# GpSimd's scale and shift of x waits for both token tiles of the next input to be split

## The chip, the cores and the metric

One core of one Trainium2 chip. The metric is the device time of the whole kernel in microseconds (us), one launch, inputs and result in HBM.

## The reference

Two layers, each of three sublayers, over x of 256 tokens by 1024 features, fp32. The six sublayers s = 0 to 5 are a gated feed-forward ("ffn"), a hybrid of window attention and a gated linear scan ("hyb"), ffn, ffn, a latent attention ("mla"), ffn. Each is wrapped like this, with shift, scale and gate out of a matrix product of a condition vector with `ada_w`:

```python
def modulated_sublayer(x, mod, g, b, fn, res_w):
    shift, scale, gate = mod[:, 0, None, :], mod[:, 1, None, :], mod[:, 2, None, :]
    y = fn(x * (1.0 + scale) + shift)
    return layer_norm(DEEPNORM_ALPHA * x + res_w * (1.0 + gate) * y, g, b)
```

The kernel makes each fp32 product out of three: each operand is split into a high part (rounded) and a low part (the rest), and high*high, low*high and high*low are summed.

## The kernel before

**Tiling.** The 256 tokens are two tiles of 128 (t = 0, 1). The weights come in slots of 128 x 2048 numbers: SyncE issues the loads into a ring of three raw buffers, ScalarE writes the high part (L771), VectorE the low part (L1042), TensorE uses both, over a ring of six. An ffn walks 11 column blocks of the hidden layer (c0 = 0 to 10), three slots each: `up` makes gate and up, VectorE multiplies (L1384, `hidden`), TensorE turns the product (`turn`, L1808), ScalarE and VectorE split it (L827 and L1389, `take_lo`), `down` adds to the result in PSUM.

**The order of the work is written out by hand, per engine.** Every engine has its own program, in one fixed order, and semaphores join them. An instruction that waits holds back all that stands behind it on its engine.

**Between two sublayers.** For each token tile, VectorE does `residual` (L1109, L1113) and `norm` (L1122 to L1128); within it GpSimd takes the power for the standard deviation (L591). L1128 leaves the normalised x in place, without the layer norm's g and b. TensorE transposes this (L1471), and VectorE (L1067) and ScalarE (L785) apply g, b, scale and shift in one step, folded into mod_G and mod_B. ScalarE rounds to hT_hi (L790, two halves), VectorE subtracts to hT_lo (L1075, two halves of 128x512), and each half raises `h_ready` by 1. The next sublayer's products wait for h_ready. VectorE's order is: residual and norm of tile 0, `enter` of tile 0 (L1067, L1075), residual and norm of tile 1, `enter` of tile 1.

**GpSimd's scale and shift.** x itself is needed with g and b as well, for the residual one sublayer later. GpSimd does that in `ln_tail`: x times ln_g (L599), plus ln_b (L601), 128x1024 each and in place, per tile; L601 raises `x_ready`. It must not start before TensorE has transposed the tile (`n_tr`).

**What stands behind ln_tail on GpSimd's queue.** Behind s = 0: masks for hyb (L628 to L649), then the distances (L655) as soon as SyncE's `mixer_inputs` have landed. Those loads (L512 to L519) wait for `x_ready` on SyncE's queue, and further weight loads stand behind them. ScalarE's L939 takes the absolute value of the distances; on ScalarE it stands ahead of the copy of the second projection's last piece (L953), and TensorE's next transposes (L1640) wait for that copy. Behind s = 1 and s = 2: `acc_start` (memset L556, bias load L559), then the loads of `ada_w` pieces (L545) into a ring of four. VectorE adds them up (L1054) from c0 = 1 on, two pieces ahead of a `split_lo` and a `take_lo`. Behind s = 3: 16 memsets for the frequencies of the rotation (L720); VectorE computes angles from them (L1263 to L1285), ScalarE the sines (L867), and behind that on ScalarE stand the squares (L871), for VectorE's and GpSimd's norms. Behind s = 4: the loads of ln_g and ln_b of the last sublayer.

Of the kernel before, what the change touches and what calls it, by code (L numbers as in the profile page):

```python
# [25 lines left out]
NT = SEQ // P  # L26
# [17 lines left out]
def build(nc, A, out):  # L44
# [11 lines left out]
    with ExitStack() as ctx:  # L56
# [3 lines left out]
        def sem(name):  # L60
            return ctx.enter_context(nc.semaphore(name))
# [129 lines left out]
        n_ready = sem("n_ready")  # L191
        n_tr = sem("n_tr")
# [3 lines left out]
        h_ready = sem("h_ready")  # L196
        pool_step = sem("pool_step")
        ln_rows_in = sem("ln_rows_in")
# [337 lines left out]
        def _(pool):  # L536
# [39 lines left out]
            def ln_tail(s):  # L576

                l, sub = divmod(s, N_SUB)
                if subs[s][0] == "hyb":

                    pool.wait_ge(ho_done, 8)
                elif subs[s][0] == "mla":

                    pool.wait_ge(o_ready, O0 + 4)
                for v, w in enumerate((A["ln_g"], A["ln_b"])):
                    pool.dma_start(ln_rows[:, v, :], w[l, sub:sub + 1, :].broadcast_to([P, D]))\
                        .then_inc(ln_rows_in, 16)
                for t in range(NT):
                    u = 2 * s + t
                    pool.wait_ge(var_ready, u + 1)  # L590
                    nc.gpsimd.tensor_tensor(rstd[:, :], var_eps[:, :], neg_half[:, :], ALU.pow).then_inc(rstd_ready, 1)  # L591
                    pool.wait_ge(n_ready, u + 1)
                    if s < last_sub:
                        pool.wait_ge(n_tr, 2 * (u + 3))
                    elif t == NT - 1:

                        break
                    pool.wait_ge(ln_rows_in, 32 * (s + 1))
                    step(nc.gpsimd.tensor_tensor(x[:, t, :], x[:, t, :], ln_rows[:, 0, :], ALU.mult))  # L599
                    step.wait()  # L600
                    nc.gpsimd.tensor_tensor(x[:, t, :], x[:, t, :], ln_rows[:, 1, :], ALU.add).then_inc(x_ready, 1)  # L601
                if s < last_sub:
                    pool.wait_ge(x_ready, 2 * (s + 1))

            for s, (kind, _, _) in enumerate(subs):
# [16 lines left out]
                if kind == "hyb":  # L622
# [57 lines left out]
                    for stage, m in hybrid_plan():  # L680
# [11 lines left out]
                        elif stage == "cum":  # L692
                            d, t = HSTEP[m]
# [3 lines left out]
                        elif stage in ("prod", "turn"):  # L697
                            d, t = HSTEP[m]
# [17 lines left out]
                if kind == "mla":  # L716
# [19 lines left out]
                    for stage, m in mla_plan():  # L736
                        if stage == "cn":
                            t = m
# [3 lines left out]
                        elif stage == "kr":  # L742
                            t = m[1]
# [6 lines left out]
                        elif stage == "uq":  # L750
                            g, t = m
# [5 lines left out]
                            x_rope = q_nat[:, t, :, 64:96]  # L757
                            rotate(x_rope, t, q_rot, [x_rope])
                ln_tail(s)


# [1149 lines left out]
```

## Time and profile before

| | |
|---|---|
| time, median of 3 runs (lowest, highest) | 1282.5 us (1280.75, 1288.55) |
| profiled execution: span from first to last instruction | 1283.1 us |
| TensorE matmul busy | 1144.7 us (89%) |
| VectorE busy | 823.9 us (64%) |
| ScalarE busy | 485.9 us (38%) |
| GpSimd busy | 234.8 us (18%) |
| TensorE's mean granted clock | 0.929 |

The profiled execution has no time of its own beside the span, so the span stands for it. Busy is the time in which an engine's instructions ran. The granted clock is a share of full speed. L12 is line 12 of the kernel; PE is TensorE, DVE is VectorE, ACT is ScalarE, POOL is GpSimd, SP is SyncE.

### The profile page before, as it was taken

To read this page: it belongs to the slowest core of one execution; us is meant where nothing else is said; L and a number is where in the kernel's file an instruction comes from. 1 tells how busy PE (TensorE), PEld (TensorE's weight loads), DVE (VectorE), ACT (ScalarE), POOL (GpSimd) and SP (SyncE) were. 2 spreads that over 40 slices of the span, in tenths; PEclk is the share of its full clock that TensorE was granted. 3 is DMA by queue.
4 is the path that set the end of the run, shared out by engine and by line. 5 is a ranking of instruction groups with operands and counts; after the bars stand their busy time and mean duration, and the time that the engine had idled before them with its cause. 6 is when DMAs were issued, how large, how long until landed. Compare 5 with 4: busy or idle time off the path is not lost. (4 is left out here: it accounts for less than half of the span.)

```text
span 1283.1 us, 14861 instructions
## 1 busy us (share of the span) xinstructions
PE 1144.7 (89%) x5205; PEld 916.4 (71%) x5205; DVE 823.9 (64%) x930; ACT 485.9 (38%) x666; POOL 234.8 (18%) x341
## 2 busy tenths in 40 slices
PE   1799999969988788999998899999889887999995
PEld 1688778747765456788787688888667676788883
DVE  6588688755565316796446799489565738444554
ACT  0543334325672103343443334343235533443440
POOL 0111221044232113210000411111143103000001
PEclk9999899879987768999999899999779998999997
DMA  8799889715451110897555399599114331665630
GB/s 317 263 318 375 299 315 357 247 31 170 132 164 52 47 33 33 312 369 275 164 191 196 125 370 356 206 364 353 41 58 148 99 99 59 204 197 197 197 98 33
DMA packets 145098, 252.28 MB, mean 197 GB/s; under 512 B 10386, under 2 KB 102802, under 8 KB 145043
## 3 DMA queue, kind: packets, MB, share of 16 engines
q1 hardware_dynamic: 124336, 176.98, 41.1%
q0 software_dynamic: 20560, 74.05, 15.4%
q8 instruction: 32, 0.52, 0.2%
q10 hardware_dynamic: 146, 0.53, 0.1%
q14 instruction: 24, 0.19, 0.0%
HBM read 250.48 MB, written 1.05 MB: 196 GB/s over the span
## 5 line engine op out<-in xcount | busy, mean ns | idle before, releaser
L1042 DVE TENSOR_TENSOR w_lo<-w_raw,w_hi 128x2048 fp32r<-128x2048 f32 (+2 forms) x164 | 364.5, 2226 | 150.8 <-ACT w_hi L771 150.6
L1476 PE MATMUL bank<-w_hi,hT_hi 128*128 128x512 f32 (+3 forms) x944 | 391.4, 415 | 32.6 <-DVE hT_lo L1075 25.0
L1479 PE MATMUL bank<-w_hi,hT_lo 128*128 128x512 f32 (+3 forms) x944 | 375.8, 398 | 0.0
L1480 PE MATMUL bank<-w_lo,hT_hi 128*128 128x512 f32 (+3 forms) x944 | 375.6, 398 | 0.0
L771 ACT ACTIVATE w_hi<-w_raw 128x2048 fp32r<-128x2048 f32 (+2 forms) x164 | 303.1, 1854 | 41.0 <-DMA w_raw<-in_ffn_w_up_dram 31.3
L1476 PEld LDWEIGHTS bank<-w_hi,hT_hi 128*128 128x128 f32 x944 | 187.2, 198 | 75.2 <-DVE hT_lo L1075 27.4
L1480 PEld LDWEIGHTS bank<-w_lo,hT_hi 128*128 128x128 f32 x944 | 185.9, 197 | 38.4
L1479 PEld LDWEIGHTS bank<-w_hi,hT_lo 128*128 128x128 f32 x944 | 187.2, 198 | 36.3 <-issue 2.3
L823 ACT ACTIVATE arena<-bank 128x256 f32<-128x256 f32 x88 | 33.8, 384 | 385.6 <-PE bank L1480 385.6
L1054 DVE SCALAR_TENSOR_TENSOR arena<-arena,cond 128x1024 f32<-128x1024 f32 x120 | 149.5, 1279 | 17.0 <-DMA arena<-in_ada_w_dram 16.9
L1476 PE MATMUL bank<-w_hi,fT_hi 128*128 128x512 f32 x352 | 143.1, 406 | 11.8 <-DVE fT_lo L1389 11.6
L1480 PE MATMUL bank<-w_lo,fT_hi 128*128 128x512 f32 x352 | 142.3, 404 | 0.0
L1479 PE MATMUL bank<-w_hi,fT_lo 128*128 128x512 f32 x352 | 141.9, 403 | 0.0
L545 POOL DMA_DIRECT2D arena<-in_ada_w_dram x120 | 63.5, 529 | 280.0 <-DVE arena L1054 254.1
L1384 DVE TENSOR_TENSOR arena<-arena,bank 128x256 f32<-128x256 f32 x88 | 36.9, 419 | 117.5 <-ACT arena L823 117.3
L1476 PEld LDWEIGHTS bank<-w_hi,fT_hi 128*128 128x128 f32 x352 | 69.0, 196 | 29.7 <-DVE fT_lo L1389 13.7
L591 POOL TENSOR_TENSOR rstd<-var_eps,neg_half 128x1 f32<-128x1 f32 x12 | 6.7, 559 | 417.4 <-DVE var_eps L1126 417.4
L1480 PEld LDWEIGHTS bank<-w_lo,fT_hi 128*128 128x128 f32 x352 | 68.9, 196 | 14.9
L1479 PEld LDWEIGHTS bank<-w_hi,fT_lo 128*128 128x128 f32 x352 | 68.9, 196 | 14.4
L827 ACT ACTIVATE fT_hi<-bank 128x256 fp32r<-128x256 f32 x88 | 33.7, 383 | 80.0 <-PE bank L1808 80.0
L1389 DVE TENSOR_TENSOR fT_lo<-bank,fT_hi 128x256 fp32r<-128x256 f32 x88 | 36.8, 418 | 21.3 <-ACT fT_hi L827 21.3
L1075 DVE TENSOR_TENSOR hT_lo<-arena,hT_hi 128x512 fp32r<-128x512 f32 x24 | 43.5, 1835 | 2.3 <-ACT hT_hi L790 1.0
(204 smaller groups left out, 958.3 us busy)
## 6 DMA issues: line engine op xcount, KB each, us to landing
arena<-in_ada_w_dram POOLq DMA_DIRECT2D x128, 512.0 KB, 6.1
w_raw<-in_ffn_w_gate_dram SPq DMA_DIRECT2D x88, 512.0 KB, 4.8
w_raw<-in_ffn_w_up_dram SPq DMA_DIRECT2D x88, 512.0 KB, 5.8
w_raw<-in_ffn_w_down_dram SPq DMA_DIRECT2D x88, 512.0 KB, 4.8
w_raw<-in_hyb_w_in_dram SPq DMA_DIRECT2D x26, 512.0 KB, 4.8
arena<-in_ada_w_dram SPq DMA_DIRECT2D x16, 512.0 KB, 5.3
w_raw<-in_hyb_w_out_dram SPq DMA_DIRECT2D x8, 512.0 KB, 4.0
w_raw<-in_mla_w_out_dram SPq DMA_DIRECT2D x8, 512.0 KB, 4.0
```

The lines of the kernel that those rows point to most:

```text
L545: pool.dma_start(ada_raw[:, a % ADA_RING, :], ada[l, :, k + 4 * i, sub * 3 * D + v * D:sub * 3 * D + (v + 1) * D])\
L771: nc.scalar.activation(w_hi[:, j0 % RING, 0:n], w_raw[:, j0 % RAW, 0:n], ACT.Copy).then_inc(hi_ready, 1)
L823: nc.scalar.activation(sg[:, t, :], G[t][:, 0:CW], ACT.Silu).then_inc(silu_done, 1)
L827: nc.scalar.activation(fT_hi[:, t, :], T[t][:, 0:CW], ACT.Copy).then_inc(fT_hi_ready, 1)
L1042: nc.vector.tensor_tensor(w_lo[:, j0 % RING, 0:n], w_raw[:, j0 % RAW, 0:n], w_hi[:, j0 % RING, 0:n].bitcast(F32), ALU.subtract)\
L1054: nc.vector.scalar_tensor_tensor(out=acc[:, v * D:(v + 1) * D], in0=ada_raw[:, a % ADA_RING, :], scalar=cond[:, 1, bass.ds(k + 4 * i, 1)], ...
L1075: nc.vector.tensor_tensor(hT_lo[:, ks, t * P:(t + 1) * P], scratch[:, half * 512:half * 512 + 512].rearrange("p (k n) -> p k n", k=4), hT_ ...
L1384: nc.vector.tensor_tensor(hid[:, t, :], sg[:, t, :], G[t][:, CW:2 * CW], ALU.mult)\
L1389: nc.vector.tensor_tensor(fT_lo[:, t, :], T[t][:, 0:CW], fT_hi[:, t, :].bitcast(F32), ALU.subtract).then_inc(fT_ready, 1)
L1476: mm = nc.tensor.matmul(dst, a_hi, b_hi, start=start, stop=False)
L1479: nc.tensor.matmul(dst, a_lo, b_hi, start=False, stop=False)
L1480: return nc.tensor.matmul(dst, a_hi, b_lo, start=False, stop=stop)
```

## The change

In `ln_tail` both powers (L591) now come first, for both tiles; then come the wait for ln_g and ln_b, and the two scale-and-shift pairs. Ahead of each pair GpSimd waits for h_ready >= 2 * (2s + 4), which is the second half of tile 1's hT_lo of the next sublayer. The last sublayer keeps its old wait.

```diff
@@ -589,13 +589,16 @@
                     u = 2 * s + t
                     pool.wait_ge(var_ready, u + 1)
                     nc.gpsimd.tensor_tensor(rstd[:, :], var_eps[:, :], neg_half[:, :], ALU.pow).then_inc(rstd_ready, 1)
-                    pool.wait_ge(n_ready, u + 1)
+                pool.wait_ge(ln_rows_in, 32 * (s + 1))
+                for t in range(NT):
+                    u = 2 * s + t
                     if s < last_sub:
-                        pool.wait_ge(n_tr, 2 * (u + 3))
+                        pool.wait_ge(h_ready, 2 * (2 * s + 4))
                     elif t == NT - 1:
 
                         break
-                    pool.wait_ge(ln_rows_in, 32 * (s + 1))
+                    else:
+                        pool.wait_ge(n_ready, u + 1)
                     step(nc.gpsimd.tensor_tensor(x[:, t, :], x[:, t, :], ln_rows[:, 0, :], ALU.mult))
                     step.wait()
                     nc.gpsimd.tensor_tensor(x[:, t, :], x[:, t, :], ln_rows[:, 1, :], ALU.add).then_inc(x_ready, 1)
```

## Rows read from the trace of the kernel before

**Rows 1.** All instructions of L1075: duration ns min/median/max, first and last start:

```profile
L1075 DVE TENSOR_TENSOR hT_lo<-arena,hT_hi x24: 681/1510/2862, 40.4 to 1084.1; 128x512 fp32r<-128x512 f32 x24
```

**Rows 2.** Timeline, entry of tile 0 into sublayer 1: start us, us, engine, line:

```profile
265.37 1.51 DVE L1075 TENSOR_TENSOR hT_lo<-arena,hT_hi 128x512 fp32r<-128x512 f32 x1
...
265.37 4.30 DVE L1075 TENSOR_TENSOR hT_lo<-arena,hT_hi 128x512 fp32r<-128x512 f32 x2
...
266.06 0.63 ACT L790 ACTIVATE hT_hi<-arena 128x512 fp32r<-128x512 f32 x1
...
263.99 2.34 POOL L599 TENSOR_TENSOR x<-x,arena 128x1024 f32<-128x1024 f32 x1 [3.91 <-issue]
266.41 2.71 POOL L601 TENSOR_TENSOR x<-x,arena 128x1024 f32<-128x1024 f32 x1
```

**Rows 3.** Timeline, sublayer 1's start, engine by engine (brackets: idle before, releaser):

```profile
280.48 0.58 PE L1476 MATMUL bank<-w_hi,hT_hi 128*128 128x256 f32 x1 [3.09 <-DVE hT_lo L1075]
...
279.61 0.63 ACT L790 ACTIVATE hT_hi<-arena 128x512 fp32r<-128x512 f32 x1
...
282.67 0.34 SPq L512 DMA_DIRECT2D arena<-in_hgrn_lb_logits_dram  x1
...
290.40 1.42 POOL L655 TENSOR_TENSOR arena<-arena,pos_col 128x256 int32<-128x256 int32 x2 [2.81 <-DMA arena<-in_hgrn_norm_w_dram]
...
294.35 0.62 ACT L939 ACTIVATE arena<-arena 128x512 f32<-128x512 int32 x1
297.49 0.60 ACT L953 ACTIVATE arena<-bank 128x512 f32<-128x512 f32 x1 [2.52 <-PE bank L1480]
...
298.14 1.10 PE L1640 MATMUL bank<-ident,arena 128*128 128x128 f32 x8 [0.69 <-ACT arena L953]
```

**Rows 4.** Timeline, GpSimd and VectorE at one time in sublayer 1:

```profile
299.92 3.23 DVE L1042 TENSOR_TENSOR w_lo<-w_raw,w_hi 128x2048 fp32r<-128x2048 f32 x1 [1.54 <-ACT w_hi L771]
...
298.47 5.84 POOL L668 TENSOR_TENSOR arena<-arena 128x512 f32<-128x512 f32 x3 [0.63 <-DVE arena L1140]
```

**Rows 5.** Timeline, sublayer 2's start, and L545's DMA issues between 510 and 540 us:

```profile
507.32 1.09 PE L1471 MATMUL bank<-ident,x 128*128 128x128 f32 x8 [0.32 <-DVE x L1128]
...
514.17 4.48 DVE L1042 TENSOR_TENSOR w_lo<-w_raw,w_hi 128x2048 fp32r<-128x2048 f32 x2
...
510.97 2.73 POOL L601 TENSOR_TENSOR x<-x,arena 128x1024 f32<-128x1024 f32 x1
...
517.53 0.55 POOL L545 DMA_DIRECT2D arena<-in_ada_w_dram  x1 [0.21 <-issue]
...
528.48 2.48 DVE L1054 SCALAR_TENSOR_TENSOR arena<-arena,cond 128x1024 f32<-128x1024 f32 x2
...
533.08 0.42 DVE L1389 TENSOR_TENSOR fT_lo<-bank,fT_hi 128x256 fp32r<-128x256 f32 x1
...
535.89 0.39 PE L1476 MATMUL bank<-w_hi,fT_hi 128*128 128x512 f32 x1
...
DMA to landing us min/median/max: 4.8/5.6/9.0
```

**Rows 6.** Timeline, sublayer 3's start (TensorE, VectorE):

```profile
716.24 1.09 PE L1471 MATMUL bank<-ident,x 128*128 128x128 f32 x8 [1.17 <-DVE x L1128]
...
737.12 2.48 DVE L1054 SCALAR_TENSOR_TENSOR arena<-arena,cond 128x1024 f32<-128x1024 f32 x2
```

**Rows 7.** Timeline, sublayer 4's (mla) start, engine by engine:

```profile
940.38 0.59 POOL L720 MEMSET freq<- 128x1 f32 x16
...
943.76 0.26 ACT L867 ACTIVATE rot<-angle 128x64 f32<-128x64 f32 x1 [5.84 <-DVE angle L1285]
...
950.40 1.22 DVE L1042 TENSOR_TENSOR w_lo<-w_raw,w_hi 128x1024 fp32r<-128x1024 f32 x1
...
953.78 1.97 PE L1541 MATMUL bank<-ident,arena 128*128 128x128 f32 x8 [0.28 <-DVE kr_nat L1305]
```

**Rows 8.** Windows of TensorE: stretch, its length, busy, granted clock (0.50 means 1.2 GHz):

```profile
498.80:504.10 5.30, 5.29 (x13) 0.50 0.00 0
```

## The prediction

> **What bounds the kernel now.** I read the busy shares first: TensorE's matmuls fill 89% of the span, so the time is TensorE's work plus the stretches in which it waits. The lines of the page name one wait above the others: L1476's first product of a sublayer waits for hT_lo (L1075). I then took L1075 by itself [rows 1]: 24 instructions of one shape take from 0.68 to 2.86 us, median 1.51. Equal work of such unequal length is waiting inside the instruction. The timeline of one entry shows on what [rows 2]: L1075's first half starts at 265.37 while L599 runs on GpSimd (to 266.33), and ends 0.55 us after that; then L601, which had started at 266.41, takes 2.71 instead of L599's 2.34, and the pair of L1075 ends at 269.67, 0.55 us after L601. The two engines take turns, each holding the other off for a whole instruction. The last view was the timeline of each of the five entries, for what stands behind `ln_tail` on GpSimd and when somebody waits for it [rows 3, 5, 7]. It decides this case.
>
> **Part one: hT_lo is freed.** With GpSimd idle L1075 costs its minimum, 0.68. The first half is ready 1.51 - 0.68 = 0.83 us earlier. The second half needs L790's second output (266.69), so it ends at 267.4 instead of 269.67: 2.27 us earlier, and VectorE goes on with tile 1's residual and norm that much sooner. What reaches TensorE differs by place:
> - Sublayer 1: TensorE waits for tile 1 anyway, so 2.27 arrive at tile 1's transposes and 0.83 more at its first product [rows 3]: 3.1 us.
> - Sublayer 2: TensorE is busy with `up` of tile 0 until 0.32 us before tile 1's transposes [rows 5]: 0.83 + 0.32 = 1.15. Tile 1's hT_lo is not waited for, since `down` comes between. Sublayer 4 repeats this pattern; there tile 1's first half (0.83) counts too.
> - Sublayer 3: idle 1.17 [rows 6]: 0.83 + 1.17 = 2.0.
> - Sublayer 5: about 0.8, only the first half.
> - The powers (L591) of both tiles ahead of the pairs cost nothing: they wait for VectorE in both orders.
>
> **Part two: GpSimd's four instructions move behind the second half of tile 1.** They are 4 x 2.34 us plus gaps, 9.8 us, where before only the second pair was left at that time. And they now meet VectorE's split of the next weight slots (L1042, 2.2 us each, two SBUF operands, 4.48 for two undisturbed [rows 5]). No row of before has this pair of shapes together; the nearest has L668, three instructions in 5.84 us, against one L1042 of 3.23 instead of 2.24 [rows 4]. So they take turns there as well: each w_lo that falls in lengthens GpSimd's series by up to 2.2. Bounds are 0 and 2.2 per w_lo; I take 2.2 where VectorE is ready.
>
> The Trainium skill (SBUF — State Buffer, Who interferes with whom) says that a VectorE instruction with two SBUF inputs and a GpSimd instruction that reads SBUF exclude each other for the whole instruction; a mere sharing of bandwidth would give the lower bound of each place below. The turns in the trace speak for the rule.
>
> Who waits behind these four:
>
> *Sublayer 1.* The last half of hT_lo ends at 280.24 - 2.27 + 0.7 = 278.7 (280.24 is L790's end [rows 3]). Four instructions and one w_lo bring x_ready to 290.5; before it was 282.64, just ahead of SyncE's L512 at 282.67 [rows 3]. So mixer_inputs start 7.8 us later; L655, which waited 2.81 us for them, comes at 298.2 and ends at 299.6. ScalarE's L939 had no wait (it ran at 294.35); now it stands at its place in ScalarE's order until 299.6. Behind it is L953, 0.5 us later, and TensorE's L1640 0.65 after L953's start: about 300.85 instead of 298.14. The gain of 3.1 is eaten, and 2.7 us are lost: **+2.7**. With no turns taken, x_ready is 2.2 earlier: +0.5.
>
> *Sublayer 2.* hT_lo's end: L1042 follows it at 514.17 now [rows 5]; less 1.15 and some 2.0 of lock wait, 511.1. Four instructions and three w_lo: 16 us, 527.1. From L601's end (513.70) to the first L545 (517.53) are 3.8 us of memset and bias load [rows 5], so the first piece is issued at 530.9 and lands 5.6 us later, at 536.5. VectorE wants it in L1054 at 528.48 now: 8.1 us late. L1389 stands behind, ends at 533.50, and TensorE takes its result at 535.89 [rows 5]: 2.4 us of cover. **+5.7** there, the entry's gain already counted. Bounds: landing 4.8 to 9.0 us gives +4.9 to +9.1; with no turns GpSimd is 6.2 earlier and little is left, about 0 to +1.
>
> *Sublayer 3* repeats it with a head start larger by 0.85 and L1054 at 737.12 [rows 6], 14.5 instead of 14.8 us after L601's end: 7.5 - 2.4 = **+5.1**. The second loop of pieces there, and the loads after the first four, are gated by VectorE's own progress and shift with it.
>
> *Sublayer 4.* The frequencies (L720) start as soon as ln_tail ends, 940.38 [rows 7]. VectorE's angles wait for them, ScalarE waited 5.84 us in front of L867 [rows 7], and squares, norms and the copies of kr stand behind that. No w_lo falls in. Against sublayer 1's 7.8, that is 2.2 less, and 1.2 more for the smaller head start (1.1 for 2.3): 6.8 us later. L1042 now ends at 951.62 [rows 7], then 958.4; with two short copies behind it, L1541 starts at 958.8 instead of 953.78: **+5.0**. VectorE is idle there, so this is the surest term.
>
> *Sublayer 5.* Nothing on GpSimd is wanted before 1268 us; the w_lo that are delayed have some 3 us in hand. **-0.8**.
>
> **The clock.** After an idle stretch TensorE ran 5.3 us at a granted clock of 0.50, 1.2 GHz [rows 8], which costs a stage bound by TensorE up to 2.5 us. Three of the new waits (sublayers 1 to 3) stand where it now runs at full clock; each costs between 0 and 2.5. I take half, **+3.6** in all, since VectorE is itself late behind two of them.
>
> **The sum.** 2.7 + 5.7 + 5.1 + 5.0 - 0.8 + 3.6 = 21.3 us, on the span of 1283.1, which is 0.6 above the median of the runs: 1282.5 + 21.3, so 1304.
>
> **Rivals.**
> - *The freed hT_lo is all that counts.* If nothing behind ln_tail is on a path, the entries give -3.1 - 1.15 - 2.0 - 1.9 - 0.8 = -9 us: 1273.5. For it: GpSimd is busy only 18%, and the waits removed are real. Against it: each of the rows L939, L867 and L1054 shows its engine with under 8 us in hand. The Trainium skill (same page, Summary: rules for kernel authors) advises to schedule whichever of the two is off the critical path; read for this change it would give this case. Chance 0.12.
> - *The second queue is covered, the others not.* GpSimd's series is not lengthened by w_lo, or pieces land early, so that sublayers 2 and 3 lose nothing: 0.5 + 0.5 + 0 + 5.0 - 0.8 = +5, 1288. For it: landing as short as 4.8 us, a cover of 2.4. Chance 0.13.
> - *It is worse.* Pieces land in 9 us (+3.4 twice) and each wait brings its full slow stretch (+3.9 more): 1315. Decides if the loads of weights fall together with the late pieces. Chance 0.10.
> - *The wait does nothing*, if GpSimd came late to it anyway: it starts L599 at 263.99 now, before the first half of tile 0 is even written [rows 2]. Chance 0.01.
>
> **How the numbers follow.** The forecast has 0.64, its own range 1297 to 1312. The range 1288 to 1316 takes in the covered and the worse case and leaves out the first rival. Of single runs (1280.75 to 1288.55) I hold that under 1% can't be told from no change. 1% slower is 1295.3: forecast and worse case, with a little of the edge taken off, 0.73. Within 1% are both milder cases, 0.25. Faster by 1% needs more than the first rival's 9 us: 0.02.
>
> **What the changed profile would show.** L1075's instructions near 0.7 us, save none. L599 and L601 in four, about 16 us, between 511 and 527 in sublayer 2, with L1042 stretched beside them. TensorE waiting some 6 us for ScalarE's L953 ahead of L1640, some 7 for L1389 at c0 = 1 in sublayers 2 and 3, and 5 to 7 ahead of L1541. VectorE's L1054 waiting for the piece's DMA near 8 to 9 us, twice. The prediction is wrong if L1054's wait is under 3 us, if L939 finds its input ready, or if GpSimd's four take 10 us in sublayer 2.

## The result and the profile after

The changed kernel takes 1307.9 us (median of 4 runs, 1301.0 to 1314.1), beside 1285.3 us for the kernel before in the same rounds (4 runs, 1280.75 to 1288.55). The ratio is 1.0171, with a 95% interval of 1.0132 to 1.021. The profiled execution has a span of 1307.8 us, 24.7 more than before; this section accounts for these 24.7. From L599 on the line numbers are 3 higher than before (L1075 is L1078 now).

First the wait that the change was to remove. This is the line of hT_lo, with what waited for it:

```profile
L1078 DVE TENSOR_TENSOR hT_lo<-arena,hT_hi x24: 680/692/693, 39.5 to 1108.2; 128x512 fp32r<-128x512 f32 x24
...
  POOL x L602: 32.9, 5
```

All 24 instructions take 0.68 to 0.69 us, none is held up any more (1.51 in the median before, [rows 1]). The second row is the price: GpSimd now stands idle 32.9 us in five waits in front of L602. The timeline of sublayer 1's start shows both:

```profile
264.04 0.58 PE L1479 MATMUL bank<-w_hi,hT_hi 128*128 128x256 f32 x1 [2.27 <-DVE hT_lo L1078]
...
276.79 2.37 POOL L602 TENSOR_TENSOR x<-x,arena 128x1024 f32<-128x1024 f32 x1 [6.59 <-DVE hT_lo L1078]
...
284.04 4.33 POOL L604 TENSOR_TENSOR x<-x,arena 128x1024 f32<-128x1024 f32 x1
...
283.32 2.79 DVE L1045 TENSOR_TENSOR w_lo<-w_raw,w_hi 128x2048 fp32r<-128x2048 f32 x1 [6.68 <-ACT w_hi L774]
...
288.40 0.34 SPq L512 DMA_DIRECT2D arena<-in_hgrn_lb_logits_dram  x1
...
296.07 2.13 POOL L658 TENSOR_TENSOR arena<-arena,pos_col 128x256 int32<-128x256 int32 x2 [1.42 <-DMA arena<-in_hgrn_norm_w_dram]
...
298.23 0.63 ACT L942 ACTIVATE arena<-arena 128x512 f32<-128x512 int32 x1 [8.93 <-POOL arena L658]
...
298.76 0.58 ACT L956 ACTIVATE arena<-bank 128x512 f32<-128x512 f32 x1
...
299.40 1.97 PE L1643 MATMUL bank<-ident,arena 128*128 128x128 f32 x8 [7.10 <-ACT arena L956]
```

TensorE's first product waits 2.27 instead of 3.09 [rows 3]. Then read the chain downward by its brackets. The last of the four instructions takes 4.33, because L1045 holds it off. SyncE's L512 follows at 288.40 (282.67 before), then GpSimd's distances, then ScalarE's L942, which waits 8.93 where it had not waited. L956 stands behind it, and TensorE waits 7.10 where it had waited 0.69 [rows 3].

Sublayer 2, the other queue:

```profile
513.57 2.38 POOL L602 TENSOR_TENSOR x<-x,arena 128x1024 f32<-128x1024 f32 x1 [7.26 <-DVE hT_lo L1078]
516.03 4.32 POOL L604 TENSOR_TENSOR x<-x,arena 128x1024 f32<-128x1024 f32 x1
520.32 4.44 POOL L602 TENSOR_TENSOR x<-x,arena 128x1024 f32<-128x1024 f32 x1
524.84 4.32 POOL L604 TENSOR_TENSOR x<-x,arena 128x1024 f32<-128x1024 f32 x1
529.22 2.68 POOL L556 MEMSET arena<- 128x3072 f32 x1
...
533.01 1.88 POOL L545 DMA_DIRECT2D arena<-in_ada_w_dram  x3 [0.22 <-issue]
...
514.53 7.97 DVE L1045 TENSOR_TENSOR w_lo<-w_raw,w_hi 128x2048 fp32r<-128x2048 f32 x2 [1.11 <-ACT w_hi L774]
...
537.28 2.48 DVE L1057 SCALAR_TENSOR_TENSOR arena<-arena,cond 128x1024 f32<-128x1024 f32 x2 [7.59 <-DMA arena<-in_ada_w_dram]
...
542.43 0.79 PE L1479 MATMUL bank<-w_hi,fT_hi 128*128 128x512 f32 x1 [5.18 <-DVE fT_lo L1392]
```

The four take 15.6 us (513.57 to 529.16) and the two w_lo 7.97 instead of 4.48 [rows 5]: the turns that L1075 was freed from are taken here. The pieces of ada_w are issued after that, VectorE waits 7.59 for the first, and TensorE 5.18 for the L1392 behind it. In sublayer 3 the same wait of L1057 is 6.58, and TensorE's behind it 3.78. Sublayer 4:

```profile
957.08 2.37 POOL L602 TENSOR_TENSOR x<-x,arena 128x1024 f32<-128x1024 f32 x1 [7.01 <-DVE hT_lo L1078]
...
966.72 0.59 POOL L723 MEMSET freq<- 128x1 f32 x16
...
970.10 0.26 ACT L870 ACTIVATE rot<-angle 128x64 f32<-128x64 f32 x1 [13.89 <-DVE angle L1288]
...
978.20 1.12 PE L1544 MATMUL bank<-ident,arena 128*128 128x128 f32 x4 [8.22 <-DVE kr_nat L1308]
```

No w_lo falls in, so these four take 9.6 us, but ScalarE waits 13.89 instead of 5.84 for the angles and TensorE 8.22 instead of 0.28 [rows 7].

**Where the 24.7 us lie.** I cut TensorE's time at the start of tile 0's transposes into each sublayer. The windows of after (stretch, its length, matmuls busy, granted clock):

```profile
260.70:496.74 236.04, 200.22 (x932) 0.81 0.27 90
496.74:715.79 219.05, 205.89 (x889) 0.94 0.64 221
715.79:940.55 224.76, 210.87 (x925) 0.95 0.73 259
940.55:1093.44 152.89, 123.00 (x648) 0.87 0.28 92
1093.44:1307.80 214.36, 190.15 (x852) 0.96 0.43 142
```

Before, the cuts lie at 262.78, 494.62, 703.57, 921.33 and 1067.13, with 196.70, 199.66, 207.75, 122.13 and 194.67 us busy. Length less busy is idle. The matmuls are the same in number (one record more or less), so a difference in busy time is a difference in clock:

| us against before | start | sub 1 | sub 2 | sub 3 | sub 4 | sub 5 | sum |
|---|---|---|---|---|---|---|---|
| TensorE idle | +0.1 | +0.7 | +3.9 | +3.9 | +6.2 | +2.9 | +17.7 |
| TensorE busy (clock) | -2.2 | +3.5 | +6.2 | +3.1 | +0.9 | -4.5 | +7.0 |
| both | -2.1 | +4.2 | +10.1 | +7.0 | +7.1 | -1.6 | +24.7 |

The stretch before the first cut runs the same code in every kernel of this study. Over the twelve other profiles it came out between 5.4 us shorter and 0.7 longer than before, most of it in the busy row (-5.9 to +0.2), and its idle row scatters by 2.7. The later stretches scatter too. Each of these ranges is over kernels that have the same code in that stretch: sublayer 1 with the old order came out at -2.6 to +0.6 against before, with the new order at +4.2 to +6.9; sublayer 3 with the new order at +7.0 to +11.5; sublayer 4 with the new order at +5.1 to +7.1. So a difference of under some 3 to 4 us between single profiles of one stretch shows nothing by itself.

### The profile page after: what moved, and what is told of

It reads as the page before. It is cut to its first block, busy times and chain, and to the rows that moved or that the text cites. A ratio compares the mean times of both kernels' runs of the same rounds, so it can differ in the third digit from the quotient of the medians.

```text
span 1307.8 us, 14855 instructions
## 1 busy us (share of the span) xinstructions
PE 1151.8 (88%) x5205; PEld 921.3 (70%) x5205; DVE 814.5 (62%) x930; ACT 486.4 (37%) x666; POOL 250.9 (19%) x341
## 4 chain that ended last, share of the span: by engine, by line
PE 62%; DVE 13%; issue 7%; ACT 7%; DMA 5%; POOL 5%; SPq 0%; DVEq 0%; POOLq 0%; ACTq 0%
PE bank L1479 17%; PE bank L1482 17%; PE bank L1483 17%; DMA arena<-in_ada_w_dram 4%; DVE w_lo L1045 3%; ACT w_hi L774 2%; POOL x L604 2%; POOL x L602 2%; PE bank L1456 2%; PE bank L1811 1%; PE bank L1750 1%; PE bank L1464 1%; DVE arena L1365 1%; PE bank L1753 1%; PE bank L1474 1%
## 5 line engine op out<-in xcount | busy, mean ns | idle before, releaser
L1045 DVE TENSOR_TENSOR w_lo<-w_raw,w_hi 128x2048 fp32r<-128x2048 f32 (+2 forms) x164 | 380.0, 2321 | 158.5 <-ACT w_hi L774 158.3
L1057 DVE SCALAR_TENSOR_TENSOR arena<-arena,cond 128x1024 f32<-128x1024 f32 x120 | 149.7, 1280 | 30.6 <-DMA arena<-in_ada_w_dram 30.6
L545 POOL DMA_DIRECT2D arena<-in_ada_w_dram x120 | 63.5, 529 | 268.1 <-DVE arena L1057 242.6
L591 POOL TENSOR_TENSOR rstd<-var_eps,neg_half 128x1 f32<-128x1 f32 x12 | 6.7, 557 | 435.8 <-DVE var_eps L1129 435.8
L1392 DVE TENSOR_TENSOR fT_lo<-bank,fT_hi 128x256 fp32r<-128x256 f32 x88 | 36.9, 419 | 23.4 <-ACT fT_hi L830 23.4
L1811 PE MATMUL bank<-ident,arena 128*128 128x128 f32 x176 | 35.8, 286 | 12.7 <-DVE arena L1387 12.6
```

Source lines behind the costliest of these rows:

```text
L545: pool.dma_start(ada_raw[:, a % ADA_RING, :], ada[l, :, k + 4 * i, sub * 3 * D + v * D:sub * 3 * D + (v + 1) * D])\
L1045: nc.vector.tensor_tensor(w_lo[:, j0 % RING, 0:n], w_raw[:, j0 % RAW, 0:n], w_hi[:, j0 % RING, 0:n].bitcast(F32), ALU.subtract)\
L1057: nc.vector.scalar_tensor_tensor(out=acc[:, v * D:(v + 1) * D], in0=ada_raw[:, a % ADA_RING, :], scalar=cond[:, 1, bass.ds(k + 4 * i, 1)], ...
L1392: nc.vector.tensor_tensor(fT_lo[:, t, :], T[t][:, 0:CW], fT_hi[:, t, :].bitcast(F32), ALU.subtract).then_inc(fT_ready, 1)
L1811: mm = nc.tensor.transpose(T[t][:, q * P:(q + 1) * P], hid[:, t, q * P:(q + 1) * P], ident[:, :])
```

## The experiments

All cuts of time below are made in this way, in one profile of each kernel; lines may be numbered a few higher. Whole times are given with the ratio and its interval where the kernel was run in rounds. Diffs are against the changed kernel, unless they say otherwise.

**No pairs.** The scale and shift of x are left out in sublayers 0 to 4; `x_ready` is raised after the wait.

```diff
                         pool.wait_ge(h_ready, 2 * (2 * s + 4))
+                    if s < last_sub:
+                        pool.sem_inc(x_ready, 1)
+                        continue
```

> Left out: GpSimd's scale and shift of x by ln_g and ln_b in sublayers 0 to 4 (x stays without them for the residual); x_ready is raised when the new wait is over. Theory Q (the loss is what is queued behind the four instructions on GpSimd): no time is spent in front of the queue, so only the freed hT_lo is left; against before -3.1 in sublayer 1, -1.2, -2.0, -1.9, -0.8 in 2 to 5, together -9 us, 1276. Theory W (the late wait itself, or the powers put first, costs something whatever GpSimd does after it): it stays slower than before, over 1290. Theory C (mostly TensorE's clock, which falls at other places from run to run): a total anywhere between 1276 and 1290, and the same stretches at half clock in sublayers 1 to 3 as in the changed kernel.

Measured: 1276.1 us, ratio 0.9932 (0.991 to 0.9954), so 8.7 us faster than before by the ratio. The new wait itself therefore costs nothing, and all the loss comes from the four instructions at their new place. The 8.7 us are near the 9 that the first rival had put on the freed hT_lo, but they don't show its worth alone: without the pairs nothing else on VectorE is held up by them either, and the queues behind them run earlier. By sublayers 1 to 5 the one profile gives -2.4, -1.0, +1.1, -1.7 and -1.0, which is not the forecast's pattern (-2.0 was expected in sublayer 3).

**Loads first.** In sublayers 2 and 3 the memset, the bias load and the first four ada_w loads are issued ahead of the pairs.

```diff
+                if s in (1, 2):
+                    nxt = ada_plan[s + 1][0]
+                    acc_start(nxt)
+                    pool.wait_ge(h_ready, 4 * s + 8)
+                    for n in range(ADA_RING):
+                        ada_piece(nxt, n, 0)
                 pool.wait_ge(ln_rows_in, 32 * (s + 1))
...
+                        if s in (2, 3) and loop == 0:
+                            for n in range(ADA_RING, 24):
+                                ada_piece(nxt, n % 12, n // 12)
+                            continue
```

> The changed kernel, with the memset, the bias load and the first four loads of ada_w pieces of sublayers 2 and 3 ahead of the four instructions instead of behind them. Theory Q: L1057's waits for the piece (7.6 and 6.6 us) go to under 1 us; sublayer 2 falls from +10.1 (against before, entry to entry) to between -1.2 and +1, sublayer 3 from +7.0 to between -2 and +1; sublayers 1 and 4 stay at +4.2 and +7.1; in all 1308 - 17, about 1291. Theory L (what hurts is that the split of the weights takes 8.0 instead of 4.5 us beside the four instructions): sublayers 2 and 3 stay above +4 each, total over 1300.

Measured: 1303.3 us, one run; about 1291 was expected. Sublayer 2 fell from +10.1 to 0.0, and VectorE's waits for pieces there from 7.6 to 1.1 us in all. That settles sublayer 2: the pieces, issued late, are its cost; w_lo is still stretched (6.69 us for two) and delays nobody that TensorE waits for. Sublayer 3 stayed at +7.2 (idle +2.8, clock +4.4). Part of this the experiment made itself, in its timeline:

```profile
720.12 2.65 POOL L556 MEMSET arena<- 128x3072 f32 x1
720.20 3.12 DVE L1141 TENSOR_SCALAR x<-x,mean_var,rstd 128x1024 f32<-128x1024 f32 x1 [0.67 <-POOL rstd L591]
...
723.38 1.97 PE L1484 MATMUL bank<-ident,x 128*128 128x128 f32 x8 [3.64 <-DVE x L1141]
```

The memset now starts right behind the second power and holds VectorE's normalisation off: 3.12 instead of 0.81 us, in front of the transposes. In sublayer 2 the same happens (3.13 us at 511.27), but TensorE is busy there and waits only 0.84.

**Frequencies first.** The 16 memsets of L723 go ahead of the pairs of s = 3.

```diff
+                if s == 3:
+                    for n in range(16):
+                        op = nc.gpsimd.memset(freq[:, n:n + 1], float(np.float32(10000.0) ** np.float32(-n / 16)))
+                    op.then_inc(freq_ready, 1)
                 pool.wait_ge(ln_rows_in, 32 * (s + 1))
```

> The changed kernel, with the 16 memsets of freq in sublayer 4 ahead of the four instructions. Theory Q: VectorE's angles and ScalarE's sines are on time, but the power for the norms (L743) still stands behind the four; it comes at the end of the series instead of 5.1 us after it. TensorE's wait ahead of its transposes of c falls from 8.2 to about 3 us, sublayer 4 from +7.1 to about +2; total about 1303. If the frequencies were not what held sublayer 4: no change there, the wait stays at 8.

Measured: 1311.0 us, one run; about 1303 was expected. TensorE's wait for kr_nat fell from 8.22 to 5.49 us, where about 3 was expected. Its timeline shows why it fell no further:

```profile
961.99 7.20 DVE L1270 TENSOR_SCALAR angle<-freq,arena 128x16 f32<-128x16 f32 x4
...
981.32 1.97 PE L1544 MATMUL bank<-ident,arena 128*128 128x128 f32 x8 [5.49 <-DVE kr_nat L1308]
```

The frequencies are now there in time and VectorE starts on the angles at once. But it now does so beside GpSimd's four instructions (961.98 to 971.6), and they hold it off: four small products of 128x16 take 7.20 us, where the kernel before needs 0.65, and the two of L1274 behind them 2.42 instead of 0.27. ScalarE still waits 12.02 us in front of L870 (13.89 in after). So the late frequencies can't be the larger part of the term: taking them away won 2.7 us of a wait that had grown by 7.9, and the pairs themselves, on VectorE's angles, keep most of the rest. By the table sublayer 4 gave +2.7 (idle +4.9, clock -2.2) instead of +7.1; with the code of after it gave +5.2 in "loads first" and +5.1 in "absolute value late" (waits for kr_nat 7.20 and 7.26), so 2.4 us or more are gained.

The total doesn't show it, since sublayer 1, whose code is that of after, came out at +6.8 instead of +4.2. Sublayer 2, also unchanged, repeated its +10.1 (idle +3.9, clock +6.2).

**Absolute value late.** ScalarE's L942 goes behind ScalarE's copies of q, and so no longer stands ahead of the copy L956.

```diff
-                        elif stage == "dist":
-                            act.wait_ge(diff_ready, 2)
-                            nc.scalar.activation(dist[:, :, :], dist[:, :, :].bitcast(I32), ACT.Abs).then_inc(dist_abs, 1)
...
+                            act.wait_ge(diff_ready, 2)
+                            nc.scalar.activation(dist[:, :, :], dist[:, :, :].bitcast(I32), ACT.Abs).then_inc(dist_abs, 1)
```

> The changed kernel, with ScalarE's absolute value of the distances moved behind its copies of q (stage qk), so that it no longer stands ahead of the copy of the second projection. Theory Q: TensorE's 7.1 us ahead of its transposes of q fall to under 1.5 us, and the stretch at half clock after them goes; sublayer 1 from +4.2 to about -2; total about 1302. If GpSimd's masks or SyncE's late weight load (slot 5) hold sublayer 1 by themselves, TensorE waits 4 us or more at its next use, and sublayer 1 stays above +2.

Measured: 1309.6 us, one run; about 1302 was expected. TensorE's timeline in sublayer 1:

```profile
293.94 1.09 PE L1642 MATMUL bank<-ident,arena 128*128 128x128 f32 x8 [0.69 <-ACT arena L953]
...
304.75 0.70 PE L1659 MATMUL bank<-arena 64*128 64x256 f32 x4 [3.80 <-DVE arena L1151]
```

The wait of 7.10 is gone, back at 0.69, so ScalarE's order was its cause. Half of it comes back 11 us later, at L1659, which needs VectorE's work on what this chain delivers. Sublayer 1 went to +0.6, where three profiles with the code of after gave +4.2, +6.8 and +6.9; -2 was expected. Sublayer 3 came out at +11.5, of which +6.3 is clock, with the code of after: again the scatter.

**Write only.** The pairs are replaced by four pairs of memsets of about their length, into ln_rows: same queue time, no reads. x keeps no scale and shift.

```diff
+                    if s < last_sub:
+                        for m in range(2):
+                            step(nc.gpsimd.memset(ln_rows[:, :, :], 0.0))
+                            step.wait()
+                            step(nc.gpsimd.memset(ln_rows[:, 0, 0:660], 0.0))
+                            step.wait()
+                        pool.sem_inc(x_ready, 1)
+                        continue
```

> The changed kernel, with GpSimd's four instructions of sublayers 0 to 4 replaced by memsets of about the same length into the space of ln_g and ln_b (x's scale and shift are left out). They read nothing from SBUF. Theory Q with turns: without reads VectorE's w_lo and these memsets run beside each other, so the series is 9.8 us and the two w_lo after the entry take 4.5 us. x_ready comes 2 us earlier (sublayer 1 about +2 against before instead of +4.2), the pieces of ada_w 6 us earlier in sublayer 2 and 4 to 5 in sublayer 3 (L1057's wait 7.6 falls to 1 to 3, so sublayer 2 is near -1 and sublayer 3 near 0 apart from the clock), and sublayer 4, where no w_lo falls in, keeps its +7. Theory S (the two engines share bandwidth, or the order on GpSimd alone counts): lengths as in the changed kernel, all four sublayers unchanged.

Measured: 1295.0 us, one run. The timeline of sublayer 2:

```profile
511.78 1.81 POOL L604 MEMSET arena<- 128x2048 f32 x1 [5.96 <-DVE hT_lo L1086]
512.77 4.50 DVE L1053 TENSOR_TENSOR w_lo<-w_raw,w_hi 128x2048 fp32r<-128x2048 f32 x2 [1.11 <-ACT w_hi L782]
...
521.46 0.65 POOL L606 MEMSET arena<- 128x660 f32 x1
...
532.01 1.29 DVE L1065 SCALAR_TENSOR_TENSOR arena<-arena,cond 128x1024 f32<-128x1024 f32 x1 [3.12 <-DMA arena<-in_ada_w_dram]
```

Two w_lo beside writes take 4.50, as if alone, and GpSimd's series keeps its length, 10.3 us (511.78 to 522.1). In sublayer 4, where no w_lo falls in, the same eight memsets take 10.3 us as well. So it is GpSimd's reads that meet VectorE's two inputs. The Trainium skill says this of a GpSimd instruction that only writes (SBUF — State Buffer, Who interferes with whom), and the rows agree. Sublayers 2 and 3 fell to +2.3 and +1.4, while sublayer 4, where no w_lo falls in, stayed at +6.6. The turns with w_lo, which delay the pieces, are thus nearly 8 of sublayer 2's 10 us in these profiles, 2.7 of it waiting and 5.1 clock; the mere delay is some 2. In sublayer 1 L512 is issued at 286.69 instead of 288.40 and TensorE waits 5.84 instead of 7.10 there; the stage's +4.2 lies within the scatter of the new order.

**Multiply only.** L604 is left out in sublayers 0 to 4: x gets no shift, and the series is half as long.

```diff
+                    if s < last_sub:
+                        nc.gpsimd.tensor_tensor(x[:, t, :], x[:, t, :], ln_rows[:, 0, :], ALU.mult).then_inc(x_ready, 1)
+                        continue
```

> The changed kernel, with the addition of ln_b (L604) left out in sublayers 0 to 4, so that GpSimd's series is two instructions instead of four. Theory Q: each chain behind it moves earlier by 4.8 us and the w_lo no longer taken turns with: the frequencies of sublayer 4 come 2.0 us later than before instead of 6.8, TensorE's 8.2 us ahead of the transposes of c fall to about 3; L956's wait of 7.1 in sublayer 1 to about 1; L1057's waits to under 1. Total within 6 us of the kernel before. If only the first instruction of the series hurts (the wait itself), nothing moves.

Measured: 1282.6 us, one run, about before's own time. With half the series, sublayers 1 to 4 give -4.1, +2.5, +4.4 and -0.4, together +2.4. TensorE still waits 2.35 for kr_nat (0.28 before, 8.22 after). So by this one profile two instructions, about 5 us, cost the queues little, and it is the 10 to 16 us of four that they charge for.

**Per tile.** Each pair waits for its own tile's hT_lo alone; otherwise the order is that of before.

```diff
                 for t in range(NT):
...
+                    pool.wait_ge(n_ready, u + 1)
                     if s < last_sub:
-                        pool.wait_ge(h_ready, 2 * (2 * s + 4))
+                        pool.wait_ge(h_ready, 2 * (u + 3))
```

> The kernel before, with GpSimd's wait for tile t only moved from the transposes to the second half of the same tile's hT_lo, so that tile 0's pair runs beside the residual and norm of tile 1, and only tile 1's pair stands ahead of the queue. Theory Q: the queue comes 2.0 us later than before at most, nearly covered everywhere; the entries win 0.8 on each first half, but the two L1113 (both operands in SBUF) and L1128 of tile 1 now take turns with tile 0's pair, which gives back up to 2.3. Total -3 to +2 us against before. Theory W (the wait for h_ready is bad by itself): +10 or more.

Measured: 1301.1 us, ratio 1.0109 (1.0059 to 1.016). It was expected within a few us of before, and is 14 us slower, which is what its rival theory (the wait is bad by itself) had put at 10 or more; but "no pairs" has the wait and is faster than before. By sublayers 1 to 5 the profile gives +3.9, +2.5, +3.9, +4.3 and +3.1. The timeline of the entry into sublayer 1 shows what was overlooked:

```profile
265.73 0.69 DVE L1075 TENSOR_TENSOR hT_lo<-arena,hT_hi 128x512 fp32r<-128x512 f32 x1 [0.66 <-ACT hT_hi L790]
...
266.56 2.39 POOL L599 TENSOR_TENSOR x<-x,arena 128x1024 f32<-128x1024 f32 x1 [7.47 <-issue]
267.73 4.51 DVE L1113 SCALAR_TENSOR_TENSOR x<-x,arena 128x512 f32<-128x512 f32 x2
269.03 2.67 POOL L601 TENSOR_TENSOR x<-x,arena 128x1024 f32<-128x1024 f32 x1
...
275.41 0.90 PE L1471 MATMUL bank<-ident,x 128*128 128x128 f32 x3 [5.84 <-DVE x L1128]
```

hT_lo is free, and the next instruction of VectorE with two inputs in SBUF, tile 1's residual L1113, takes its place: 4.51 for what takes 1.28 alone. Tile 1's normalisation (L1128) then starts at 274.54, before at 274.56, though the entry came 1.0 us earlier here. The gain is paid back at once, and the delay of the second pair remains: L512 is issued at 285.92, before at 282.67 [rows 3]. In later entries tile 1's transposes wait longer than before (3.2 instead of 1.2 us in sublayer 3, 3.1 in sublayers 4 and 5), and so do those behind kr_nat (2.54 instead of 0.28). How much of the 14 us is due to each of the two effects, no run takes apart.

**Chosen.** The late wait only for s = 1, 2 and 4, with the first loads ahead of the pairs for s = 1 and 2 (here behind the wait, so that the memset meets no normalisation); the old order for s = 0 and 3.

```diff
+                late = s in (1, 2, 4)
...
+                if s in (1, 2):
+                    nxt = ada_plan[s + 1][0]
+                    pool.wait_ge(h_ready, 4 * s + 8)
+                    acc_start(nxt)
+                    for n in range(ADA_RING):
+                        ada_piece(nxt, n, 0)
...
```

> The new order only where the queue behind it can be moved or is empty: sublayers 2, 3 (entries behind s = 1, 2) and 5 have the late wait, in the first two with memset, bias load and the first four loads of ada_w ahead of the four instructions (the memset now after the wait, so that it doesn't meet VectorE's L1128); the entries behind s = 0 and s = 3 keep the old order. Theory Q: -1.2, -2.0 and -0.8 us, nothing else: 4 us faster than before, 1280, with L1075 at 0.69 in those three places. Theory L (the w_lo stretched by the turns reach TensorE): 0 to +4.

Measured: 1283.9 us, ratio 0.9991 (0.9965 to 1.0017), so the 4 us that were expected did not come. By sublayers +0.1, +2.8, +0.7, 0.0 and -2.0. TensorE's idle time in sublayer 2 is 1.3 us below before's, as the removed wait should give, and its busy time 4.1 above. Most of the 4.1 is a stretch at half clock at c0 = 5 that the profile of before happens to lack, as the next section shows. The order costs nothing any more, and no gain is shown.

**Pairs late.** For s = 1 and 2 the pairs go behind the last load of ada_w that the next sublayer issues (in sublayer 3 that is the end of its second series of pieces). For s = 4 no such loads follow, and the pairs simply have the late wait. s = 0 and 3 are as before. The memset of `acc_start` waits for hT_lo in sublayers 2 and 3, so that it does not meet the normalisation.

```diff
+            def late_pairs(s):
+                pool.wait_ge(h_ready, 4 * s + 8)
+                pool.wait_ge(ln_rows_in, 32 * (s + 1))
+                for t in range(NT):
...
+                        if s > 0 and loop == 0:
+                            pool.wait_ge(h_ready, 4 * s + 4)
                         acc_start(nxt)
...
                             for n in range(12):
                                 ada_piece(nxt, n, i)
...
+                if s in (2, 3, 5):
+                    late_pairs(s - 1)
```

> Sublayers 2, 3 and 5: GpSimd's four instructions go behind all that is queued there (in sublayers 2 and 3 behind the last load of ada_w, some 80 and 165 us after the entry; x_ready is wanted 110 and 200 us after it), the memset for ada_w waits for the last half of hT_lo. The entries behind s = 0 and s = 3 keep the old order. Theory Q: nothing is late any more, and the w_lo of the first blocks meet nobody: -1.2, -2.0 and -0.8 us (in the run with the late wait and empty queue, sublayer 5 gave 1.0 to 2.0), 4 to 5 us faster than before, ratio 0.996 to 0.997. Theory C (differences of this size are the clock's): the idle time of TensorE falls by 3 to 5 us, but the ratio's interval includes 1.

Measured: 1294.3 us, ratio 1.0073 (1.0044 to 1.0103), where 0.996 to 0.997 was expected. The timeline of sublayer 2:

```profile
578.04 3.27 POOL L611 TENSOR_TENSOR x<-x,arena 128x1024 f32<-128x1024 f32 x1
579.31 4.15 DVE L1057 TENSOR_TENSOR w_lo<-w_raw,w_hi 128x2048 fp32r<-128x2048 f32 x1
581.39 4.32 POOL L613 TENSOR_TENSOR x<-x,arena 128x1024 f32<-128x1024 f32 x1
583.71 6.42 DVE L1069 SCALAR_TENSOR_TENSOR arena<-arena,cond 128x1024 f32<-128x1024 f32 x2
...
594.74 2.47 DVE L1069 SCALAR_TENSOR_TENSOR arena<-arena,cond 128x1024 f32<-128x1024 f32 x2
```

There is nothing on GpSimd behind the pairs here that anyone needs, and sublayers 2 and 3 still lose 9.1 and 8.5 us. VectorE works without a gap at this place, adding pieces and splitting weights, all with two inputs: the two L1069 take 6.42 beside the pairs and 2.47 without, and each w_lo about 2 more. TensorE then waits 4.46 us for the fT_lo behind them.

**Pairs in slack.** Against the kernel before: the pairs of s = 1 go behind the last step of the modulation in sublayer 2, where VectorE had stopped adding pieces; those of s = 4 as in "pairs late"; s = 0, 2 and 3 as before. The memset's wait in sublayers 2 and 3 is that of "pairs late" too.

```diff
+                    if s in (1, 4):
+                        continue
...
+                        if s > 0 and loop == 0:
+                            pool.wait_ge(h_ready, 4 * s + 4)
...
+                if s == 2:
+                    pool.wait_ge(mods_ready, 4)
+                if s in (2, 5):
+                    late_pairs(s - 1)
```

> Where the four instructions stand beside VectorE's ada_w pieces (pairs_late: sublayers 2 and 3 +9.1 and +8.5) each of the two-operand VectorE instructions waits out one of theirs. Here sublayer 2's four wait until these pieces are done and the next modulation is ready (about 607 us), when VectorE has 2 to 5 us of waiting in each block; the entries behind s = 0, 2 and 3 keep the old order, the one behind s = 4 is late. Theory T (VectorE's slack where the four instructions fall decides): sublayer 2 goes from +9.1 to between -1.2 and +1, sublayer 3 to about 0, sublayer 5 -1 to -2; no wait of TensorE for L1389 over 2.2 us in sublayer 2; total 2 to 3 us faster than before, ratio about 0.998. If pairs_late lost by something else in sublayer 2 (the memset's new wait, the later start of the pieces), +3 or more stay there.

Measured: 1281.9 us, ratio 0.9963 (0.9933 to 0.9992): the one complete kernel of this study that beats both, if only just. GpSimd's timeline of sublayer 2:

```profile
600.40 2.39 POOL L611 TENSOR_TENSOR x<-x,arena 128x1024 f32<-128x1024 f32 x1 [26.14 <-DVE mod_B L1112]
...
607.68 2.40 POOL L613 TENSOR_TENSOR x<-x,arena 128x1024 f32<-128x1024 f32 x1
```

The same four instructions, 22 us later than in "pairs late", keep their undisturbed lengths: 9.7 us in place of 14.3. One w_lo still meets the last of them (4.23 us at 607.99), and TensorE waits 0.67 behind it. Sublayer 2 gives +0.2 instead of +9.1, which is the point of the experiment. Where the whole kernel gains its 0.4% the profile doesn't show. Sublayers 1 to 5 give -2.6, +0.2, +4.1, +1.4 and -1.8: the first and the fourth have before's code, and sublayer 3, where about 0 was expected, lost most, half of it in a wait of 2.10 us for an fT_lo behind pieces of ada_w, 150 us after the entry.

**Only mla.** Against the kernel before: the late wait for s = 3 alone.

```diff
+                    if s == 3:
+                        continue
...
+                if s == 3:
+                    pool.wait_ge(h_ready, 4 * s + 8)
+                    pool.wait_ge(ln_rows_in, 32 * (s + 1))
+                    for t in range(NT):
...
```

> The late wait in one place alone, the entry behind s = 3 (into the latent attention), all else as before. Theory Q: the frequencies come 6.8 us later, sublayer 4 costs +5 to +7, nothing elsewhere but what the clock does; ratio 1.004 to 1.005. If the places are not independent (a loss in one is the consequence of an earlier one), sublayer 4 loses less than +3 by itself.

Measured: 1290.2 us, ratio 1.0048 (1.0019 to 1.0077). Sublayer 4 gives +7.1 and its wait for kr_nat 8.17, as in after (+7.1, 8.22), so this term stands by itself and does not come from the others. In us the ratio is 6.2.

## Why the prediction was right, point by point

The forecast was +21.3 us; the profile shows +24.7, the medians +22.6. The mechanism was right: the pairs take turns with w_lo behind the new wait, and all three queues behind them come late. That the number came out so near is in part luck. Without the clock the forecast summed to +17.7, and TensorE's idle time grew by 17.7 over the whole kernel; but by sublayers it was 2.7, 5.7, 5.1, 5.0 and -0.8 against 0.7, 3.9, 3.9, 6.2 and 2.9, three terms too large by 5.0 together and two too small by 4.9. Some of the prediction's own steps are off by 0.1 to 0.4 us (9.8 + 3 x 2.2 is 16.4 and not 16; 278.7 + 9.8 + 2.2 is 290.7 and not 290.5; 536.5 - 528.48 is 8.0 and not 8.1); none of this changes the outcome.

- **The lock on hT_lo** was read rightly. L1078 takes 0.69 everywhere. The worth of 9 us that the entries were summed to is not shown by itself; without the pairs the kernel gains 8.7 us in all.
- **The turns with w_lo** were forecast at 16 us for GpSimd's four instructions in sublayer 2, which take 15.6. "Write only" shows that the turns, more than the delay, make the cost there.
- **Sublayer 1.** x_ready was put 7.8 us later; L512 is 5.7 later on the clock and 7.8 counted from the entry, which came 2.1 earlier. Counted so, L1643 comes 3.3 later (+2.7 forecast). The wait of 7.1 had been put at some 6. "Absolute value late" shows the link by ScalarE's order, and shows too that half of the wait is owed to VectorE behind it; the prediction had followed the chain no further than L953. The three profiles with this code gave the stage +4.2, +6.8 and +6.9, against 2.7 forecast plus some 1.2 of clock, so the term was probably short.
- **Sublayers 2 and 3.** +5.7 and +5.1 were forecast without clock. The first product behind the late L1392 comes 6.5 later, 4.4 counted from the entry. The idle time grew by 3.9 in each. VectorE's waits for the piece are 7.59 and 6.58 (8 to 9 forecast) and TensorE's behind L1392 5.18 and 3.78 (some 7 forecast), so the delay was put too high and more of it was covered. "Loads first" shows that the pieces are the cause in sublayer 2. For sublayer 3 no run shows it apart from the clock.
- **Sublayer 4** was called the surest. TensorE waits 8.22 (5 to 7 forecast); L1544 comes 5.2 later counted from the entry (+5.0 forecast). Another 1.9 us are lost behind it; idle grows by 6.2, and by 6.1 in "only mla". So the term is short by 1 to 2 us. The prediction gave all of it to the late frequencies; "frequencies first" shows that with these in time the pairs hold off VectorE's angles instead, and most of the wait stays.
- **Sublayer 5**: -1.6 measured, -0.8 forecast, within the scatter.
- **The clock** is the term that was mis-sized: +3.6 was forecast for three waits in sublayers 1 to 3, half of the bound for each. Each in fact brought its whole stretch at half clock. Windows of TensorE after (stretch, length, busy, granted clock):

```profile
299.30:305.00 5.70, 5.60 (x20) 0.51 0.73 267
542.40:547.40 5.00, 4.97 (x12) 0.52 1.00 348
606.30:611.00 4.70, 4.70 (x35) 0.75 0.38 129
611.00:615.50 4.50, 4.50 (x11) 0.51 0.50 175
```

The first two lie right behind the waits of 7.10 and 5.18. Busy time times what is missing to a clock of 1.00 gives 2.7 and 2.4 us; behind sublayer 3's wait (759.8 to 765.2, 5.19 busy at 0.50) it is 2.6. In the kernel before TensorE runs at 1.00 at all three places (298.1 to 303.8, 535.8 to 540.8, 735 to 760). Together that is an estimate of 7.7 us instead of 3.6. There is another slow stretch in sublayer 2 (below), and part is given back elsewhere (-4.5 in sublayer 5, -2.2 at the start), so the whole kernel shows +7.0.

The other two windows have no new wait near them: they lie 64 us behind the last one, at c0 = 5, in the 32 column products (L1456) for the next modulation and in what follows. Before, the same place runs at 1.00:

```profile
601.00:605.00 4.00, 4.00 (x19) 1.00 0.76 256
```

It would be wrong to put this on the change. Of the thirteen profiles eleven have a stretch at half clock behind these products in sublayer 2, and only before and "loads first" have none. "Only mla" has it, whose code up to there is that of before:

```profile
598.00:602.00 4.00, 4.00 (x13) 0.58 0.85 262
```

In the same way of counting it costs 1.7 us in "only mla" and 3.4 in after. So up to 3.4 of sublayer 2's +6.2 in the clock row is something that the profile of before happened to be without. Why the clock falls at this place, and why not every time, is open.

The rivals: "the freed hT_lo is all" holds for the kernel without pairs alone, and there only in its total; "the second queue is covered" fell with the wait of 7.59, and "the wait does nothing" with L602's 32.9 us. "It is worse" was half right: each wait did bring its full slow stretch (+4.1 more than forecast, +3.9 in the rival), but there were no landings of 9 us. L545's first piece was in use 4.3 us after its issue (533.01 to 537.28).

## What to carry to other kernels

Before a step on an in-order queue is made to wait, list what stands behind it on that queue and on the queues that wait for it, each with the us in hand; here loads, pieces and frequencies stood behind a step whose own result is wanted by nobody but SyncE's loads in sublayer 1 so soon, and the change cost 22 us. When two engines exclude each other, moving one does not remove the exclusion but picks another victim: look at which instructions lie at the new place, those with two inputs and also small ones from SBUF to SBUF ("frequencies first"). The best place of those tried was the one where the other engine had idle time ("pairs late" against "pairs in slack"). And before a slow stretch of one trace is put on a change, look for it in a second kernel with the same code at that place.

## What the runs showed of the hardware that was not expected

- A write-only memset on GpSimd leaves VectorE's two-input w_lo alone (4.50 for two) but stretches its one-input normalisation from SBUF to SBUF, from 0.81 to 3.12, as shown in "loads first". GpSimd's reading and writing instructions hold one-input products off too, however small: four of 128x16 took 7.20 instead of 0.65 in "frequencies first". So there are two kinds of interference: reads against a second input, and, as far as these two cases show, any access against one-input instructions from SBUF to SBUF. The Trainium skill has the second too, for tensor_scalar in a mode that uses two ports (SBUF — State Buffer, Who interferes with whom); that L1141 and L1270 run in that mode no row shows.
- The exclusion alternates between two back-to-back streams, so both are stretched: in sublayer 2 the four of GpSimd by 5.9 us (9.7 alone in "pairs in slack", 15.6 here), the first two w_lo by 3.5.
- TensorE's clock can fall to 0.51 in a stretch that has no idle time (4.50 of 4.50 us busy above), behind column products; it did so in eleven of thirteen profiles, at one and the same place.
